# Half-zeroed queries on 64-row tiles, masks inside the products, a new item order and identity transposes in a two-layer transformer block

## What is computed

```python
# 'dsa': 4 heads of 64, one key and value head; an index score picks 64 keys per query
score = einsum('bqh,bqhs->bqs', w_idx, relu(einsum('bqhd,bsd->bqhs', q_idx, k_idx)))
_, idx = lax.top_k(where(mask, score, -inf), 64)
# 'diff': 4 heads, each with two maps of dimension 32
logits = einsum('bqhcd,bshcd->bhcqs', qb, k) * 32 ** -0.5
p = masked_softmax(logits, mask)
a = p[:, :, 0] - lam * p[:, :, 1]
# 'mla': 8 heads, logits over 64 + 32 dimensions, queries and keys from compressed rows
logits = (einsum('bqhd,bshd->bhqs', q_nope, k_nope) + einsum('bqhd,bsd->bhqs', q_rope, k_rope)) * 96 ** -0.5
```

## Time and profile before

| what | us |
|---|---|
| median of 3 runs (1602.86 to 1602.99) | 1602.93 |
| the profiled execution | 1598.53 |
| its span, first to last instruction | 1596.7 |
| TensorE busy | 1550.6 |
| VectorE busy | 1266.9 |
| ScalarE busy | 1039.3 |
| GpSimd busy | 58.7 |

### The profile page before, as it was taken

One profiled execution on the slowest core, in us unless ns is written; L12 is line 12 of the kernel. 1 busy time (PEld: TensorE's weight loads), 2 busy tenths in 40 slices (PEclk: granted clock), 3 DMA queues, 4 the chain that ended last, 5 costly groups with the idle time before them and its releaser, 6 DMA issues.

```text
span 1596.7 us, 18779 instructions
## 1 busy us (share of the span) xinstructions
PE 1550.6 (97%) x7086; PEld 1252.5 (78%) x7086; DVE 1266.9 (79%) x1564; ACT 1039.3 (65%) x1328; POOL 58.7 (4%) x128
## 2 busy tenths in 40 slices
PE   7989999999899989999999999999999999999996
PEld 6867788888787778888888888888888888888885
DVE  6477655555548769899899899899899889999995
ACT  5444544443446457787788787787778778778774
POOL 2210000000113000000000000000000000000000
PEclk9978999999998789999999999999999999999998
DMA  7503454554252119999999999999999999999992
GB/s 282 191 2 106 177 197 172 182 187 160 86 180 106 54 67 372 373 359 360 341 358 365 334 357 370 343 354 368 337 364 356 343 358 362 345 369 362 358 359 95
DMA packets 181821, 431.61 MB, mean 270 GB/s; under 512 B 3808, under 2 KB 10336, under 8 KB 181728
## 3 DMA queue, kind: packets, MB, share of 16 engines
q1 hardware_dynamic: 180720, 428.01, 73.4%
q10 hardware_dynamic: 1008, 2.36, 0.4%
HBM read 429.31 MB, written 1.05 MB: 270 GB/s over the span
## 4 chain that ended last, share of the span: by engine, by line
PE 93%; DVE 4%; ACT 1%; issue 1%; POOL 0%; DMA 0%; DVEq 0%; SPq 0%; POOLq 0%
PE pair L828 50%; PE work L828 32%; PE pair L893 3%; PE work L804 2%; PE pair L804 2%; PE work L966 1%; PE work L815 1%; PE work L1069 1%; DVE arena L1519 0%; PE work L1083 0%; PE work L1084 0%; DMA h<-in_x 0%; DVE arena L1536 0%; DVE nmax L1550 0%; PE pair L896 0%
## 5 line engine op out<-in xcount | busy, mean ns | idle before, releaser
L1460 DVE TENSOR_TENSOR w_lo<-ring,w_hi 128x1024 fp32r<-128x1024 f32 (+3 forms) x810 | 967.1, 1215 | 198.5 <-ACT w_hi L1166 184.5
L1166 ACT ACTIVATE w_hi<-ring 128x1024 fp32r<-128x1024 f32 (+3 forms) x810 | 846.1, 1055 | 332.6 <-PE pair L828 177.2
L828 PE MATMUL pair<-w_hi,hnT_hi 128*128 128x512 f32 x672 | 269.2, 401 | 2.9 <-DVE hnT_lo L1468 2.6
L828 PE MATMUL pair<-w_hi,hnT_lo 128*128 128x512 f32 x672 | 265.9, 396 | 0.0
L828 PE MATMUL pair<-w_lo,hnT_hi 128*128 128x512 f32 x672 | 265.8, 396 | 0.0
L828 PE MATMUL work<-w_hi,hidT_hi 128*128 128x512 f32 x552 | 218.8, 396 | 2.6 <-DVE hidT_lo L1711 1.4
L828 PE MATMUL work<-w_lo,hidT_hi 128*128 128x512 f32 x552 | 218.1, 395 | 0.0
L828 PE MATMUL work<-w_hi,hidT_lo 128*128 128x512 f32 x552 | 218.1, 395 | 0.0
L828 PE MATMUL pair<-w_hi,xU_hi 128*128 128x512 f32 x448 | 179.4, 401 | 0.0
L828 PE MATMUL pair<-w_hi,xU_lo 128*128 128x512 f32 x448 | 177.0, 395 | 0.0
L828 PE MATMUL pair<-w_lo,xU_hi 128*128 128x512 f32 x448 | 176.9, 395 | 0.0
(11 more groups left out here) (205 smaller groups left out, 1373.9 us busy)
## 6 DMA issues: line engine op xcount, KB each, us to landing
ring<-in_moe_w_gate SPq DMA_DIRECT2D x56, 2048.0 KB, 9.2
ring<-in_moe_w_up SPq DMA_DIRECT2D x56, 2048.0 KB, 9.7
ring<-in_moe_w_down SPq DMA_DIRECT2D x56, 2048.0 KB, 8.9
ring<-in_dense_w_gate SPq DMA_DIRECT2D x7, 2048.0 KB, 7.8
ring<-in_dense_w_up SPq DMA_DIRECT2D x7, 2048.0 KB, 7.8
ring<-in_dense_w_down SPq DMA_DIRECT2D x7, 2048.0 KB, 8.0
ring<-in_w_in SPq DMA_DIRECT2D x4, 2048.0 KB, 9.5
ring<-in_w_out SPq DMA_DIRECT2D x4, 2048.0 KB, 9.4
```

The lines of the kernel that those rows point to most:

```text
L828: mm = pe.matmul(b, lhs[x_part][k + kk], w[w_part][:, kk, :], start=(first and kk == 0 and i == 0), stop=(last and kk == 1 and i == 2))
L1166: return act.activation(o, i, ACT.Copy)
L1460: dve.tensor_tensor(lo, raw, hi.bitcast(F32), ALU.subtract).then_inc(lo_done, 1)
```

## The change

- `diff` logits: two units share 64 rows. BT writes the scaled queries twice, into `diff_queries(t)` (over the first 512 columns of `pb`), once with the odd heads' rows multiplied by zero and once with the even ones' (`half_scale`, a scale per partition). A product takes 64 rows of those and of the keys. The mask of both maps is one product of 2 * 64 columns.
- `mla` masks: `qcT` and `kcT` get two further rows each, which GpSimd writes in `mask_rows` behind N1.1 (both in layer 0, those of `qcT` again in layer 1), and the product takes 98 rows. Its mask products go.
- FL: 16 places a layer in which TensorE does three transposes of the identity into the bank of the next job; twelve more stand ahead of layer 0.
- Both lists are new. PC's squares and the set-up values use other memory.

The diff, with the lists cut to the lines that matter most:

```diff
-N1.0 N2.0 N1.1 N2.1 X.0.1 SP.0 X.0.0 SP.1 SP.2 SP.3 X.1.0 X.1.1 AN SP.4 PC.0 SP.5 C1.0 SP.6 SP.7 PC.1 C2.0
-R.kr.1 PA.1 PA.0 C1.1 C2.1 CT.0 SP.8 CT.1 SP.9 QC.0.1 KV.0.1 R.kr.0 SP.10 SP.11 KV.0.0 QC.0.0 R.c.0 PB.1
...
-TK.0.3 U.diff.0.0 AT.0 U.diff.1.1 CB.diff.1.2 AT.1 TK.0.4 TP.diff.1.2 TK.1.0 CB.diff.0.0 O.diff.1.2 TK.0.5
-O.diff.0.3 TP.diff.0.0 CB.diff.1.1 U.diff.0.1 O.diff.0.0 U.mla.0.0 TK.0.6 TK.1.1 CB.diff.0.1 TP.diff.1.1
-CB.mla.0.0 O.diff.1.1 TP.mla.0.0 TK.0.7 U.dsa.0.0 TP.diff.0.1 U.diff.1.0 O.mla.0.0 TK.1.2 U.dsa.0.1 O.diff.0.1
...
-O.diff.1.3 TP.mla.1.0 U.dsa.1.0 U.dsa.1.1 CB.mla.1.1 D2.0 CB.mla.1.0 O.mla.1.0 O.mla.1.1 D1.1 TP.dsa.1.0
-OT.0.1 TP.dsa.1.1 OT.0.0 SP.22 SP.23 CB.dsa.1.0 D2.1 O.dsa.1.0 CB.dsa.1.1 O.dsa.1.1 SP.24 SP.25 SP.26 SP.27
-WO.0.0 OT.1.0 OT.1.1 WO.0.1 NF1.0 NF2.0 WO.1.0 SP.28 SP.29 SP.30 WO.1.1 XF.0.1 NF1.1 XF.0.0 NF2.1
...
+N1.0 N2.0 N1.1 N2.1 X.0.1 FL.6 SP.0 X.0.0 SP.1 SP.2 FL.8 SP.3 X.1.0 X.1.1 SP.4 AN SP.5 SP.6 PC.0 C1.0 SP.7
+PC.1 R.kr.0 C1.1 C2.0 C2.1 PA.1 SP.8 PA.0 R.kr.1 CT.0 SP.9 CT.1 QC.0.0 SP.10 QC.0.1 SP.11 KV.0.1 KV.0.0 SP.12
...
+TP.mla.1.2 FL.15 U.idx.0.0 R.b.1 U.idx.0.1 O.mla.0.1 TP.mla.1.0 U.idx.0.2 U.idx.0.3 R.b.0 TK.0.0 R.i.1 BT.0
...
+TP.diff.1.3 U.idx.1.2 U.idx.1.3 U.dsa.0.0 U.dsa.0.1 U.diff.1.1 O.diff.0.0 FL.0 TK.1.0 FL.10 FL.11 TP.dsa.0.0
+FL.2 D1.0 CB.dsa.0.1 CB.diff.1.1 CB.dsa.0.0 O.diff.1.3 TP.dsa.0.1 D2.0 AT.1 O.dsa.0.0 U.diff.1.0 TP.diff.1.1
+O.dsa.0.1 TK.1.1 CB.diff.1.0 FL.9 OT.0.0 OT.0.1 TK.1.2 TK.1.3 U.diff.1.2 TK.1.4 TP.diff.1.0 O.diff.1.1 TK.1.5
+CB.diff.1.2 SP.26 WO.0.0 TK.1.6 TK.1.7 SP.27 TP.diff.1.2 U.dsa.1.0 U.dsa.1.1 O.diff.1.2 O.diff.1.0 D1.1 WO.0.1
+CB.dsa.1.1 FL.5 TP.dsa.1.0 CB.dsa.1.0 D2.1 TP.dsa.1.1 O.dsa.1.0 NF1.0 O.dsa.1.1 NF2.0 OT.1.1 OT.1.0 XF.0.0
+SP.28 SP.29 SP.30 FL.1 FL.12 WO.1.0 WO.1.1 XF.0.1 FL.13 NF1.1 NF2.1 FL.14
...
-N1.0 N2.0 X.0.0 X.0.1 SP.0 SP.1 SP.2 SP.3 N1.1 N2.1 PC.0 C1.0 X.1.1 C2.0 X.1.0 SP.4 CT.0 PC.1 KV.0.1 SP.5 SP.6
-R.kr.0 C1.1 SP.7 SP.8 KV.0.0 C2.1 SP.9 QC.0.1 QC.0.0 R.kr.1 PA.0 CT.1 PA.1 R.c.0 MK.0.0 MK.0.1 MQ.0.1 SP.10
...
+N1.0 N2.0 X.0.0 X.0.1 SP.0 N1.1 SP.1 SP.2 SP.3 N2.1 SP.4 SP.5 PC.0 X.1.0 X.1.1 SP.6 FL.2 C1.0 C2.0 PC.1 CT.0
+SP.7 C1.1 SP.8 PA.0 KV.0.1 KV.0.0 C2.1 R.kr.1 R.kr.0 PA.1 SP.9 QC.0.0 QC.0.1 CT.1 SP.10 SP.11 R.c.0 PB.1
...
+O.dsa.1.0 O.dsa.1.1 SP.25 SP.26 SP.27 OT.1.0 OT.1.1 WO.0.1 NF1.0 NF2.0 SP.28 WO.1.0 SP.29 SP.30 XF.0.0 WO.1.1
+XF.0.1 FL.11 XF.1.1 FL.7 NF1.1 XF.1.0 HS.0 FL.15 NF2.1 RT.0 RT.1 FL.3 FL.10 FL.12 HS.1 FL.14
...
-    NOT_JOBS = ("U", "R", "CB", "N1", "N2", "C1", "C2", "D1", "D2", "NF1", "NF2", "SP", "TK", "AN", "LR", "HS")
-    JOB = {}
+    NOT_JOBS = ("U", "R", "CB", "N1", "N2", "C1", "C2", "D1", "D2", "NF1", "NF2", "SP", "TK", "AN", "LR", "HS", "FL")
+    JOB, FILL = {}, {}
     for layer in range(DEPTH):
         for item in ORDER[layer]:
+            if item[0] == "FL":
+                FILL[(layer, *item)] = len(JOB)
             if item[0] not in NOT_JOBS:
                 JOB[(layer, *item)] = len(JOB)
...
-        mask_k = sb("mask_k", [P, CHUNK], BF16)
+        mask_k = sb("mask_k", [P, 2 * CHUNK], BF16)
...
-        bT = carve(4 * S).rearrange("p (k s) -> p k s", k=4)
+        bT = carve(2 * S).rearrange("p (k s) -> p k s", k=2)
+        half_scale = carve(2)
+        carve(2 * S - 2)
...
+        score_all = carve(T * S)
+        score = score_all.rearrange("p (t s) -> p t s", t=T)
...
+        def diff_queries(t):
+            return pb[:, t, 0:4 * P].rearrange("p (a m s) -> p a m s", a=2, m=2)
...
+            def mask_rows(layer):
+                for i in range(4 if layer == 0 else 0):
+                    link(pool.memset(half_scale[32 * i:32 * i + 32, i % 2:i % 2 + 1], DB ** -0.5))
+                    link(pool.memset(half_scale[32 * i:32 * i + 32, 1 - i % 2:2 - i % 2], 0.0))
+                for rows, first, value in ((qcT, 0, 1.0), (kcT, CHUNK, MASKED))[0:DEPTH - layer]:
+                    link(pool.memset(rows[DC:DC + T, :, :], 0.0))
+                    link(pool.memset(rows[DC:DC + T, :, P + first:P + first + CHUNK], value))
+                    link(pool.memset(rows[DC:DC + 1, :, P:2 * P], 0.0))
+                    link(pool.memset(rows[DC:DC + 1, :, first:first + CHUNK], value))
...
                         norm_root(("attn", layer), t)
+                        if t == T - 1:
+                            pool.wait_ge(rms_ready, norm_count(("attn", layer), t))
+                            mask_rows(layer)
...
-                n = JOB[key]
+                return bank_free(JOB[key])
+            def bank_free(n):
...
+            def turn_identity(b):
+                transposes(b, [ident[:, :] for _ in range(3)])
...
-                        r = 32 * p
-                        q, k = bT[r:r + DB, m, tile(t)], bT[r:r + DB, 2 + m, 0:nk]
+                        r = 64 * (p // 2)
+                        q, k = diff_queries(t)[r:r + 64, p % 2, m, :], bT[r:r + 64, m, 0:nk]
                     elif kind == "mla":
-                        q, k, r = qcT[0:DC, 2 * p + m, tile(t)], kcT[0:DC, 2 * p + m, 0:nk], 0
+                        q, k = qcT[0:DC + T, 2 * p + m, tile(t)], kcT[0:DC + T, 2 * p + m, 0:nk]
                     else:
                         r = 64 * p
                         q, k = aT[r:r + 64, m, tile(t)], aT[r:r + 64, 2, 0:nk]
-                    plain = kind in ("idx", "dsa")
-                    last = pe.matmul(S2[:, m, 0:nk], q, k, start=True, stop=plain)
-                    if not plain:
-                        last = pe.matmul(S2[:, m, nk - CHUNK:nk], mask_q[r:r + 1, :], mask_k[r:r + 1, :],
-                                         start=False, stop=True)
+                    last = pe.matmul(S2[:, m, 0:nk], q, k, start=(m == 0 or kind != "diff"), stop=(kind != "diff"))
+                if kind == "diff":
+                    last = pe.matmul(S2[:, :, nk - CHUNK:nk], mask_q[r:r + 1, :],
+                                     mask_k[r:r + 1, :].rearrange("p (m s) -> p m s", m=2), start=False, stop=True)
                 last.then_inc(logits_ready, 1)
...
+                    elif name == "FL":
+                        turn_identity(bank_free(FILL[key]))
...
             pe.wait_ge(consts_ready, 1)
+            for _ in range(4):
+                turn_identity(bank_free(0))
...
-                        act.activation(kcT[:, 2 * t, 0:CQ], b[:, 0:CQ], ACT.Square, accum_out=cstat[:, t, 0, 0:1])
-                        act.activation(kcT[:, 2 * t + 1, 0:CKV], b[:, CQ:CQ + CKV], ACT.Square,
+                        act.activation(cT[:, 0:2, t * P:(t + 1) * P], b[:, 0:CQ].rearrange("p (k s) -> p k s", k=2), ACT.Square,
+                                       accum_out=cstat[:, t, 0, 0:1])
+                        act.activation(cT[:, 2, t * P:(t + 1) * P], b[:, CQ:CQ + CKV], ACT.Square,
...
-                    elif name in ("BT", "AT"):
+                    elif name == "BT":
 
                         t = item[1]
                         b = job(act, key)
-                        dst, n, scale = (bT, 4, DB ** -0.5) if name == "BT" else (aT, 3, DA ** -0.5)
-                        v = b[:, 0:n * P].rearrange("p (k s) -> p k s", k=n)
-                        act.mul(dst[:, 0:2, t * P:(t + 1) * P], v[:, 0:2, :], scale)
-                        copy(dst[:, 2:n, t * P:(t + 1) * P], v[:, 2:n, :]).then_inc(out_of(key), 1)
+                        v = b[:, :].rearrange("p (k s) -> p k s", k=4)
+                        for odd in range(2):
+                            act.activation(diff_queries(t)[:, odd, :, :], v[:, 0:2, :], ACT.Copy,
+                                           scale=half_scale[:, odd:odd + 1])
+                        copy(bT[:, :, t * P:(t + 1) * P], v[:, 2:4, :]).then_inc(out_of(key), 1)
+                    elif name == "AT":
+                        t = item[1]
+                        b = job(act, key)
+                        v = b[:, 0:3 * P].rearrange("p (k s) -> p k s", k=3)
+                        act.mul(aT[:, 0:2, t * P:(t + 1) * P], v[:, 0:2, :], DA ** -0.5)
+                        copy(aT[:, 2:3, t * P:(t + 1) * P], v[:, 2:3, :]).then_inc(out_of(key), 1)
```

More of the change, by code:

```diff
@@ L69 @@
[L69 to L71 removed]
+N1.0 N2.0 N1.1 N2.1 X.0.1 FL.6 SP.0 X.0.0 SP.1 SP.2 FL.8 SP.3 X.1.0 X.1.1 SP.4 AN SP.5 SP.6 PC.0 C1.0 SP.7
+PC.1 R.kr.0 C1.1 C2.0 C2.1 PA.1 SP.8 PA.0 R.kr.1 CT.0 SP.9 CT.1 QC.0.0 SP.10 QC.0.1 SP.11 KV.0.1 KV.0.0 SP.12
+SP.13 PB.0 R.c.0 MQ.0.0 MK.0.0 SP.14 MK.0.1 MQ.0.1 QC.1.0 QC.1.1 KV.1.0 KV.1.1 PB.1 R.c.1 U.mla.0.0 MK.1.0
@@ new lines @@
+MK.1.1 SP.15 MQ.1.0 U.mla.0.3 MQ.1.1 CB.mla.0.0 U.mla.0.2 SP.16 TP.mla.0.0 PI.1 U.mla.0.1 SP.17 SP.18 PI.0
+CB.mla.0.2 SP.19 O.mla.0.0 SP.20 TP.mla.0.3 CB.mla.0.1 SP.21 SP.22 R.a.1 U.mla.1.2 R.a.0 TP.mla.0.2 CB.mla.0.3
+PK.0 U.mla.1.0 CB.mla.1.2 PK.1 O.mla.0.2 CB.mla.1.0 R.i.0 KIT.0 O.mla.0.3 SP.23 SP.24 IT.0 TP.mla.0.1
+TP.mla.1.2 FL.15 U.idx.0.0 R.b.1 U.idx.0.1 O.mla.0.1 TP.mla.1.0 U.idx.0.2 U.idx.0.3 R.b.0 TK.0.0 R.i.1 BT.0
```

(24 more changed lines are left out.)

41 lines of the change are left out of this document (14 added, 27 removed).

## The result

The changed kernel takes 1556.38 us (median of four runs, 1553.95 to 1568.28) against 1602.96; the ratio is 0.9739, 95% interval 0.9710 to 0.9768. The forecast was 1586.5, its range 1577.0 to 1600.5. The sign was right, the size too small by 30 us. The profiled execution took 1553.95 us, its span is 1552.0, the mean granted clock 0.985. It is the quickest of the four; the others had clocks of 0.983, 0.983 and 0.973.

The account below looks back on a forecast made before the run. TensorE bounds the experts' stage; in attention VectorE does at full clock, TensorE in slow stretches. 14.2 + 1.0 + 3.5 − 2.2 = 16.5 off 1598.5 gives 1582.0; with 4.4 added 1586.4, stated as 1586.5; range 1577 to 1600.5.

Parts of the forecast that it names:

- moves as a block: Experts' stage: untouched, TensorE never idle; each microsecond attention ends earlier is one of the result, nothing won behind it.
- the dense feed-forward is alike: Dense part: untouched by the change like the experts' stage, so no gain there.
- the terms for the long and the short slow pieces: Attention: full clock in two long stretches gains 14.2 us; fill and order gain 3.5 at short slow pieces.
- stay full: Both long attention stretches: the clock stays full and VectorE sets the pace, 14.2 us together, lower bound nothing.
- Layer 0's long stretch: Attention, 97 to 134 us at half clock: 31.1 us instead of 37 at full clock, a gain of 5.9.
- the prediction's own test: Profile after: a clock of 0.50 for over 20 us in either layer would show the prediction wrong.
- The short piece of layer 1's start: Slow piece 425 to 428 us: 1.5 us to win; PC.1 ahead of CT.0 shortens the 2.39 us wait by 1.0.
- three causes I gave: Attention's full clock: difference logits on 64 rows, 24 dense products among layer 0's selection rounds, three identity transposes at 16 places a layer.
- Masks of the latent heads: Attention: masks as operand rows save 0.26 us a pair; 1.0 us counted where TensorE is the bound, bounds 0 and 4.2.
- Identity transposes: Fill in attention: five uncovered places cost 2.2 us; 14.1 if no cover held, lower bound nothing.
- Difference logits: Attention: a 64-row pair with one mask product equals the 32-row pair's 1.20 us; 2.2 us either way over 16 units.
- The 0 for the order: New item lists: layer 0's moved TensorE and VectorE work cancels, nothing gained, 5 us to either side.

Follow-up runs that it names:

- E2: The changed kernel with the buffer cos moved behind w_lo, so the split weights start where they did in the kernel before: 1575.74 us, ratio 0.9866.
- E1: The kernel before with mask_k made wider and the added part unused, so the split weights start 128 bytes later: 1580.14 us, ratio 0.9876.
- E8: The changed kernel with the difference logits on 32 rows again, each map with its own mask product: 1556.37 us, ratio 0.9739.
- E4: The kernel before with the two new item lists, without identity transposes and nothing else new: 1602.93 us, ratio 1.0012.
- E3: The changed kernel without any identity transposes: 1562.52 us, ratio 0.9753.
- E7: The changed kernel's products, masks and buffers with the old item lists and no identity transposes: 1566.31 us, ratio 0.9781.
- E9: The changed kernel with the latent heads' mask products back and without the fills of the operand rows: 1565.51 us, ratio 0.9805.
- E13: A kernel of only the experts' 128x512 products, 42 per start address of the weights: one run, 0.2271 to 0.2333 us a product at five starts.
- E14: The products alone again, with w_hi, w_lo and the stationary tiles each shifted by 0 to 192 bytes: one run, 0.2267 to 0.2333 us at equal weight remainders.
- E10: The changed kernel with the 64-byte buffer wi moved behind w_lo, so the weights start at byte 171904: 1545.43 us, ratio 0.9659.

## Why the prediction was wrong

**The step that failed** is the sentence that none of the experts' work is touched and that the stage "moves as a block ... nothing can be won behind it", with "the dense feed-forward is alike". The diff shows that the instructions are the same, and that `mask_k` doubles; I read that line as a mask's shape and not as a shift of everything allocated behind it. It is worth 17.3 us in the experts and 4.5 in the dense part, 21.8 of the 44.7 in the spans, shown by removal (E2) and by itself (E1). Without it the changed kernel takes 1575.7, still just under the range: 27 us less than before, where 16.5 were forecast. No rival had it.

**Clock: near in size, wrong in place.** Twice the span times what the mean clock lacks to 1 gives the time at the slow level: 92.6 us in the kernel before and 46.6 after. What that is worth can be read off runs of one kernel: after, 46.6 us of it went with 1553.95 and 84.6 with 1568.28, so 0.38 us each; E1, 97.7 with 1578.16 and 114.1 with 1586.62, 0.52. That is a price from two pairs of runs, with clocks known to 0.001, and so an estimate. 46 us fewer are then 17 to 24; the terms for the long and the short slow pieces were 14.2 + 3.5 = 17.7. That they meet is in part luck, for the clock did not "stay full". Layer 0's long stretch went from 37 us to two short ones, the pieces behind 168 and 578 us vanished, and layer 1 kept its slow clock from 495.4 to 515.8 us, which the prediction's own test (over 20 us in either layer) just calls wrong. The short piece of layer 1's start stayed: the wait of 2.39 us ahead of CT.0 is gone, but one of 2.06 us stands ahead of PC.1, and the clock is slow from 410.0 to 413.4:

```profile
408.88 0.43 PE L864 MATMUL work<-w_hi,hnT_hi 128*128 128x416 f32 x1 [2.06 <-DVE hnT_lo L1517]
```

Layer 0 won 11.1 us in place of the 5.9 of its long stretch, layer 1 with the routing 9.7.

**Why the clock rose is only half as I said.** Of the three causes I gave, the 64 rows fell (E8, beside the fill) and the order by itself, with the dense products that it moves, fell (E4). The fill did it in part: from E3 to the changed kernel is 28 us less slow time by the medians (81 to 53) for 6 us, though the two intervals of the time overlap. The rest, from 107 us in E1 to 80 in E7 (medians), came with the new products and masks. E8 and E9 both keep the low slow time (medians 59 and 59, of clocks that vary), so neither kind alone explains it. That part stays open.

**Masks of the latent heads: mis-sized.** I took 1.0 us with an upper bound of 4.2. E9 loses 9 us by the medians, with a spread of 15 us among its runs; its two runs with the least slow time (49.9 and 43.7 us) took 1561, against 1554 to 1557.5 at 47 to 53 for the changed kernel, so 5 is the better figure, an estimate, and the bound was still too low. The step that failed is the price of a pair without its masks: I took 1.06 us from a 64-row pair that stands alone, and it is 0.87, while a pair with its masks in a row of pairs is 1.47. So a pair wins 0.60 us and not 0.26, and 16 pairs 9.7 where TensorE is the bound, which it is for part of them. In the profiles E9 is 5.3 us longer in layer 1 and 0.3 in layer 0, but the slow clock is placed differently too: in layer 1 it lasts 30.7 us in place of 20.4, in layer 0's long part 3.4 in place of 17.1. So this split does not say where the masks cost.

**Identity transposes: cost of the right order.** At 0.38 us a microsecond of slow time, the 28 us spared are worth 10.6, and 6 were seen; so by this estimate the fill costs some 4 to 5, against 2.2 in the sum. At 0.52 it would be 8 to 9. No run measures it by itself.

**Difference logits, order, GpSimd: as forecast.** The changed kernel's pair of 64 rows with its one mask product goes from 101.36 to 102.57, 1.21 us, against 1.20 before:

```profile
101.36 1.13 PE L930 MATMUL pair<-arena 64*128 64x256 f32 x4
102.42 0.22 PE L933 MATMUL pair<-mask_k,mask_q 1*128 1x128 bf16 x1
102.57 0.55 PE L836 MATMUL work<-ident 128*128 128x128 f32 x3
```

The 0 for the order was right (E4, 1.0012), with layer 0 8.2 us longer and layer 1 2.5 shorter in its profile. GpSimd has 14.3 us more work and nothing waits before CT.0.

**The ledger** (who won what, in this order of steps), by ratios to before, times 1603 us: the address 20 (E1); the products, masks and squares with the old order 15 (E1 to E7); the new order on top of them 4 (E7 to E3); the fill 2 by the ratios, 6 by the medians (E3 to after). The last two steps are within the intervals; the first two are not.

## What to carry to other kernels

When a buffer changes its size, look at what is allocated behind it before you call a stage untouched, and compare start-to-start times of the same product in both traces at the same granted clock. For a stream of fp32r products it is worth a run to place the moving operand and the stationary tiles at the same remainder of 256 bytes: here 7 us of a 990 us stage for one moved 64-byte buffer. A small product of other shape between large ones costs more than its own length (0.30 us for a mask product of 64 columns); price it in a row of the same units. And change one thing at a time: of five parts in this change one, unlisted, gave nearly half, and the 64 rows and the order by itself gave nothing that could be measured.

## What the runs showed of the hardware

- The pace of 128x512 fp32r products at the full clock depends on the starts of weights and stationary tiles relative to each other, with a period of 256 bytes: 0.2267 to 0.2344 us, 3.4%, with no other engine at work (E13, E14). The Trainium skill, "TensorE: Matmul & The Clock Gate", Part 2, "Step-by-step: what each phase is for", says that loading the next tile's weights does not take SBUF read bandwidth from the running matmul. E14 does not bear that out as far as the pace goes: moving only the tiles changes it by up to 3% (0.2267 to 0.2333). That the two reads meet in the same place of the memory would explain it, but that is argued, not shown.
- Transposes of the identity raise the share of time at the full clock in this kernel (E3 against the changed kernel, E2 and E10), and twelve of them at half speed stand directly ahead of one rise; another rise came without them.
- Products on 32 rows hold the clock as well as those on 64, with the fill in place (E8: 0.976 to 0.982 against 0.973 to 0.985).
- A mask product of one row between products of 96 rows is 0.13 us from start to start, and the product behind it 0.32 in place of 0.22; with the last ahead of it also late (0.31), the four masks of two pairs cost 1.21 us (E9 against the changed kernel).
